# A streaming encoder step: order of dense and modulation quarters in the first feed-forward, and a new sum of the modulation rows

## The reference

```python
mod = jax.nn.silu(c) @ w + b                 # w: (2048, 6 * 2048) for each layer
...
x = x + gate1 * mix
h = rms_norm(x, g_ffn[i]) * (1.0 + scale2) + shift2
x = x + gate2 * ((silu(h @ w_gate[i]) * (h @ w_up[i])) @ w_down[i])
```

## Time and profile before

| What | Value |
|---|---|
| Time, median of 3 runs | 3439.44 us (3436.16 to 3441.07) |
| Profiled execution: its time, its span | 3440.21 us, 3438.4 us |
| Busy: TensorE, VectorE, ScalarE, GpSimd | 3290.4 (96%), 2095.9 (61%), 1309.0 (38%), 140.6 (4%) us |
| Mean granted clock of TensorE | 0.981 |
| Chain of work that ended last: TensorE, VectorE, DMA, ScalarE | 87%, 5%, 4%, 3% |
| First feed-forward | 983 to 2198 us |

### The profile page before, as it was taken

One profiled execution on the slowest core, in us unless ns is written; L12 is line 12 of the kernel. 1 busy time (PEld: TensorE's weight loads), 2 busy tenths in 40 slices (PEclk: granted clock), 3 DMA queues, 4 the chain that ended last, 5 costly groups with the idle time before them and its releaser, 6 DMA issues.

```text
span 3438.4 us, 48286 instructions
## 1 busy us (share of the span) xinstructions
PE 3290.4 (96%) x20405; PEld 2983.9 (87%) x20405; DVE 2095.9 (61%) x1804; ACT 1309.0 (38%) x991; POOL 140.6 (4%) x141
## 2 busy tenths in 40 slices
PE   7999998889989999999999999769999999999999
PEld 4677776667979999999999999659999999999999
DVE  3487885556887667676776767685444443334443
ACT  3344444455453443334433343334222232232221
POOL 0000000000000000000000000010000000000000
PEclk9999999999989999999999999889999999999999
DMA  9777767877645655556555555553433433333331
GB/s 353 272 259 241 246 241 250 294 273 262 221 166 175 208 203 180 186 183 209 194 178 188 195 203 187 181 187 134 130 126 122 130 126 122 131 125 122 124 132 62
DMA packets 325817, 646.50 MB, mean 188 GB/s; under 512 B 10882, under 2 KB 13514, under 8 KB 325322
## 3 DMA queue, kind: packets, MB, share of 16 engines
q1 hardware_dynamic: 317144, 630.17, 53.6%
q10 hardware_dynamic: 8586, 15.09, 1.2%
HBM read 631.46 MB, written 14.74 MB: 188 GB/s over the span
## 4 chain that ended last, share of the span: by engine, by line
PE 87%; DVE 5%; DMA 4%; ACT 3%; issue 1%; POOL 0%; SPq 0%; ACTq 0%; DVEq 0%; POOLq 0%
PE bank L1501 23%; PE bank L1503 23%; PE bank L1502 23%; PE bank L1583 3%; PE bank L1528 3%; PE bank L1584 3%; PE bank L1585 3%; DMA raw<-in_w_ada 3%; PE bank L1688 1%; PE bank L1537 1%; PE bank L1513 1%; PE bank L1716 1%; DMA raw<-in_cache_k 0%; PE bank L1717 0%; DVE w_lo L955 0%
## 5 line engine op out<-in xcount | busy, mean ns | idle before, releaser
L955 DVE TENSOR_TENSOR w_lo<-raw,w_hi 128x2048 fp32r<-128x2048 f32 x323 | 739.1, 2291 | 901.5 <-ACT w_hi L578 901.5
L578 ACT ACTIVATE w_hi<-raw 128x2048 fp32r<-128x2048 f32 x323 | 616.1, 1914 | 1373.3 <-PE bank L1503 1180.3
L1501 PE MATMUL bank<-h_hi,w_hi 128*128 128x384 f32 x3136 | 1064.1, 339 | 31.9 <-DVE h_lo L1034 24.0
L1502 PE MATMUL bank<-h_lo,w_hi 128*128 128x384 f32 x3136 | 1052.4, 336 | 0.0
L1503 PE MATMUL bank<-h_hi,w_lo 128*128 128x384 f32 x3120 | 1048.0, 336 | 0.0
L1501 PEld LDWEIGHTS bank<-h_hi,w_hi 128*128 128x128 f32 x3136 | 592.2, 189 | 77.1 <-issue 68.7
L1502 PEld LDWEIGHTS bank<-h_lo,w_hi 128*128 128x128 f32 x3136 | 592.4, 189 | 0.0
L1503 PEld LDWEIGHTS bank<-h_hi,w_lo 128*128 128x128 f32 x3120 | 589.0, 189 | 0.0
L1501 PE MATMUL bank<-act_hi,w_hi 128*128 128x384 f32 x1408 | 473.0, 336 | 0.0
L1503 PE MATMUL bank<-act_hi,w_lo 128*128 128x384 f32 x1408 | 470.5, 334 | 0.0
L1502 PE MATMUL bank<-act_lo,w_hi 128*128 128x384 f32 x1408 | 470.5, 334 | 0.0
(11 more groups left out here) (226 smaller groups left out, 2530.6 us busy)
## 6 DMA issues: line engine op xcount, KB each, us to landing
raw<-in_w_ada SPq DMA_DIRECT2D x192, 1024.0 KB, 5.9
raw<-in_w_gate SPq DMA_DIRECT2D x88, 1024.0 KB, 5.2
raw<-in_w_up SPq DMA_DIRECT2D x88, 1024.0 KB, 5.2
raw<-in_w_down SPq DMA_DIRECT2D x88, 1024.0 KB, 5.1
raw<-in_w_qkv SPq DMA_DIRECT2D x40, 1024.0 KB, 5.2
raw<-in_cache_k SPq DMA_DIRECT2D x32, 1024.0 KB, 6.3
raw<-in_cache_v SPq DMA_DIRECT2D x32, 1024.0 KB, 7.8
raw<-in_w_o SPq DMA_DIRECT2D x15, 1024.0 KB, 5.1
```

The lines of the kernel that those rows point to most:

```text
L578: act.activation(w_hi[:, s], raw[:, s], ACT.Copy).then_inc(hi_ready, 1)
L955: dve.tensor_tensor(w_lo[:, s], raw[:, s], w_hi[:, s].bitcast(f32), ALU.subtract).then_inc(lo_ready, 1)
L1501: pe.matmul(out, w, a, start=start, stop=False)
L1502: pe.matmul(out, w, al, start=False, stop=False)
```

## The change

In the first feed-forward, the eight quarters of gate and of up come in the order dense, dense, modulation, modulation (twice), where they came dense, modulation in turn. So slots 0 and 1 hold dense quarters and slots 2 and 3 modulation quarters; the last dense up quarter is unit 13, where it was unit 14. `paired` takes the place of `mixed`, and the waits that name units follow.

In all stages, the turn of the partial rows is four transposes of 128 x 128 (`ident`), where it was four matmuls with 9 columns. VectorE then sums the four groups, and in three-piece blocks the three pieces (`tensor_reduce`, 432 elements a partition, or 144 for the early and pooling blocks), waits for that, and adds the bias. `fold` and `fold3` and the GpSimd instructions that write them go. The four units ahead of the feed-forward, in the output projection and the norm, follow the new order.

```diff
@@ SyncE, order of the transfers
             def load_mixed(W, c, layer, a):
                 for i, w in enumerate((w_gate, w_up)):
-                    for j in range(4):
-                        load_pair(W + 2 * i, j, rows(w[0, j * 512:(j + 1) * 512, ds(c * 512, 512)]), layer, a + i)
+                    for n in range(8):
+                        j = 2 * (n // 4) + n % 2
+                        dense = rows(w[0, j * 512:(j + 1) * 512, ds(c * 512, 512)])
+                        load(*unit(W + 2 * i, n), dense if n % 4 < 2 else ada_src(layer, a + i, j))
                 load_down(W + 4, 0, c)
@@ GpSimd, at the start
-            do(pool.memset(fold[:], 0.0))
-            do(pool.memset(fold3[:], 0.0))
-            for j in range(4):
-                do(pool.affine_select(out=fold[:], in_=fold[:], compare_op=ALU.not_equal, fill=1.0,
...
@@ ScalarE (VectorE has the same with lo and mid)
+            def paired(W, n):
+                W, s = unit(W, n)
+                if s < 2:
+                    hi(W, [s])
+                else:
+                    top(W, [s])
...
             def mixed_chunk(W, c, a, following, last=False):
                 for n in range(4, 10):
-                    mixed(W, n)
-                gate_out(4 * W + 7)
-                mixed(W, 10); mod_out(4 * W + 8, a, 3); mixed(W, 11)
+                    paired(W, n)
+                gate_out(4 * W + 6)
+                paired(W, 10); mod_out(4 * W + 8, a, 3); paired(W, 11)
                 for n in range(12, 16):
-                    mixed(W, n)
+                    paired(W, n)
                 dense(W, 16); dense(W, 17)
                 for m in range(4):
                     acts_hi(c, m)
@@ VectorE
-            def mod_in(a, t_bank, part=None):
+            def mod_in(a, t_bank, part=None, pieces=3):
                 m = ds(4 * (a if part is None else part), 4)
                 dve.wait_ge(ada_t, a + 1)
+                parts = bank[:, t_bank, :].rearrange("p (m j q) -> p m j q", m=4, j=4)[:, :, :, 0:pieces * NC]
+                if pieces == 1:
+                    step.mark(dve.tensor_reduce(modA[:, m, :], parts.rearrange("p m j c -> p m c j"), AX.X, ALU.add))
+                else:
+                    step.mark(dve.tensor_reduce(modA[:, m, :], parts.rearrange("p m j (r c) -> p m c j r", r=pieces), AX.XY, ALU.add))
+                own()
                 bias = par[:, m].unsqueeze(2).to_broadcast([P, 4, NC])
-                dve.tensor_tensor(modA[:, m, :],
-                                  bank[:, t_bank, 0:4 * NC].rearrange("p (k c) -> p k c", k=4),
-                                  bias, ALU.add).then_inc(ada_done, 1)
+                dve.tensor_tensor(modA[:, m, :], modA[:, m, :], bias, ALU.add).then_inc(ada_done, 1)
...
             def mixed_chunk(W, c, a, layer, r, following, last=False):
                 for n in range(4, 12):
-                    mixed(W, n)
+                    paired(W, n)
                 mod_in(a, 4)
                 for n in range(12, 16):
-                    mixed(W, n)
+                    paired(W, n)
                 dense(W, 16); dense(W, 17)
-                times_up(c, 4 * W + 15)
+                times_up(c, 4 * W + 14)
                 dense(W, 18)
                 mod_in(a + 1, 3)
@@ TensorE
-            def ada_turn(a, t_bank, weights=fold3):
+            def ada_turn(a, t_bank):
...
                 for t in range(4):
-                    last = pe.matmul(bank[:, t_bank, t * NC:(t + 1) * NC], mod[:, t * P:(t + 1) * P], weights[:], start=True, stop=True)
+                    last = pe.transpose(bank[:, t_bank, t * P:(t + 1) * P], mod[:, t * P:(t + 1) * P], ident[:])
                 last.then_inc(ada_t, 1)
...
@@ TensorE, mixed_chunk
-                    to_features(W, 2 * j, 4, h_hi, h_lo, 4 * j, j == 0, j == 3, second_half=None if j else hr + 1)
-                    if j == 0:
+                    to_features(W, 4 * (j // 2) + j % 2, 4, h_hi, h_lo, 4 * j, j == 0, j == 3, second_half=None if j else hr + 1)
+                    if j == 1:
                         pe.wait_ge(residual_taken, r)
-                    ada_sub(W, 2 * j + 1, a, j, 3)
+                    if j % 2:
+                        ada_sub(W, 2 * j, a, j - 1, 3)
+                        ada_sub(W, 2 * j + 1, a, j, 3)
...
                 ada_turn(a, 4)
-                ada_sub(W, 9, a + 1, 0, 7)
-                for j in (1, 2):
-                    to_features(W, 8 + 2 * j, 0, h_hi, h_lo, 4 * j, False, False)
-                    ada_sub(W, 9 + 2 * j, a + 1, j, 7)
-                up_tail(W, 14)
+                to_features(W, 9, 0, h_hi, h_lo, 4, False, False)
+                ada_sub(W, 10, a + 1, 0, 7)
+                ada_sub(W, 11, a + 1, 1, 7)
+                to_features(W, 12, 0, h_hi, h_lo, 8, False, False)
+                up_tail(W, 13)
+                ada_sub(W, 14, a + 1, 2, 7)
                 ada_sub(W, 15, a + 1, 3, 7)
```

More of the change, by code:

```diff
@@ L149, in encoder_step @@
         mask, _ = nxt("mask", [P, 512])
-        fold, _ = nxt("fold", [P, NC])
-        fold3, _ = nxt("fold3", [P, NC])
         mod, _ = nxt("mod", [P, 512])
@@ L633, in norm_apply @@
                     for s in BETWEEN[n][g]:
-                        (mixed if n == 1 else dense)(W, s)
+                        (paired if n == 1 else dense)(W, s)
                     norm_tiles(n, 4 * g, 4, g + 2)
@@ L832, in _ @@
                 for n in range(6, 10):
-                    mixed(W, n)
+                    (paired if i == 3 else mixed)(W, n) if n >= 8 else mixed(W, n)
                 if i < 3:
@@ L887, in _ @@
             with act.Fori(0, CHUNKS - 1) as c:
-                mixed_chunk(W_FFN0 + c * 5, c, ADA_FFN + c * 2, mixed)
+                mixed_chunk(W_FFN0 + c * 5, c, ADA_FFN + c * 2, paired)
             mixed_chunk(W_FFN0 + 5 * (CHUNKS - 1), CHUNKS - 1, ADA_FFN + 2 * (CHUNKS - 1), dense, last=True)
@@ L975, in dense, with paired @@
                 lo(W, [s])
-            def mod_in(a, t_bank, part=None):
+            def paired(W, n):
+                W, s = unit(W, n)
+                if s < 2:
+                    lo(W, [s])
+                else:
+                    mid(W, s)
+            def mod_in(a, t_bank, part=None, pieces=3):
                 m = ds(4 * (a if part is None else part), 4)
                 dve.wait_ge(ada_t, a + 1)
+                parts = bank[:, t_bank, :].rearrange("p (m j q) -> p m j q", m=4, j=4)[:, :, :, 0:pieces * NC]
+                if pieces == 1:
+                    step.mark(dve.tensor_reduce(modA[:, m, :], parts.rearrange("p m j c -> p m c j"), AX.X, ALU.add))
+                else:
+                    step.mark(dve.tensor_reduce(modA[:, m, :], parts.rearrange("p m j (r c) -> p m c j r", r=pieces), AX.XY, ALU.add))
+                own()
                 bias = par[:, m].unsqueeze(2).to_broadcast([P, 4, NC])
-                dve.tensor_tensor(modA[:, m, :],
-                                  bank[:, t_bank, 0:4 * NC].rearrange("p (k c) -> p k c", k=4),
-                                  bias, ALU.add).then_inc(ada_done, 1)
+                dve.tensor_tensor(modA[:, m, :], modA[:, m, :], bias, ALU.add).then_inc(ada_done, 1)
             def norm_coef(n, k0=0, tiles=KT):
@@ L1115, in _ @@
             dve.wait_ge(par_ready, 1)
-            mod_in(0, 7, FIRST[0])
+            mod_in(0, 7, FIRST[0], 1)
             dve.wait_ge(rs_done, 1)
@@ L1122, in _ @@
                 if g:
-                    mod_in(i, 7, FIRST[i]); early(i)
-                mod_in(i + 1, 7, FIRST[i + 1])
+                    mod_in(i, 7, FIRST[i], 1); early(i)
+                mod_in(i + 1, 7, FIRST[i + 1], 1)
                 norm_coef(0, 4 * g, 4)
@@ L1413, in dense_chunk @@
                         rows_out(s)
-            with loop(dve, 0, CHUNKS - 1, {step: 4 * ADD}) as c:
-                mixed_chunk(W_FFN0 + c * 5, c, ADA_FFN + c * 2, 0, R_FFN0 + c * 4, mixed)
+            with loop(dve, 0, CHUNKS - 1, {step: 4 * ADD + 2}) as c:
+                mixed_chunk(W_FFN0 + c * 5, c, ADA_FFN + c * 2, 0, R_FFN0 + c * 4, paired)
             mixed_chunk(W_FFN0 + 5 * (CHUNKS - 1), CHUNKS - 1, ADA_FFN + 2 * (CHUNKS - 1), 0, R_FFN0 + 4 * (CHUNKS - 1), dense, last=True)
@@ L1479, in _ @@
                 if j % 2:
-                    mod_in(ADA_POOL + j // 2, 3)
+                    mod_in(ADA_POOL + j // 2, 3, pieces=1)
                 if j >= 3 and j % 2:
@@ L1611, in _ @@
             pe.wait_ge(par_ready, 1)
-            ada_turn(0, 7, fold)
+            ada_turn(0, 7)
             pe.wait_ge(xT_dve, 6)
@@ L1619, in _ @@
             ada_block(1, 6)
-            ada_turn(1, 7, fold)
+            ada_turn(1, 7)
             def early(d, turn=None):
@@ L1628, in early @@
                     if k == 2 and turn is not None:
-                        ada_turn(turn, 7, fold)
+                        ada_turn(turn, 7)
                     kt = 4 * j + k
@@ L1941, in _ @@
                 if j % 2:
-                    ada_turn(ADA_POOL + j // 2, 3, fold)
```

(1 more changed line is left out.)

## The result

The changed kernel takes 3486.12 us (median of 4 runs, 3480.70 to 3492.09), the kernel before 3437.80 (4 runs): a ratio of 1.0139, 95% interval 1.012 to 1.0159. It is slower, by 48 us; forecast were 3499, with a range of 3463 to 3515 (the forecast's own, without the rivals, was 3488 to 3508). The profiled execution took 3492.09 us with a span of 3490.3, 51.9 more than the one of before; forecast +59.9.

What follows compares the result with a forecast made beforehand. TensorE was taken as the bound. Against the profiled 3440.2 us, -22 - 4.8 + 55 + 26.4 + 2 + 3.3 = +59.9 gave 3500, forecast as 3499; own range 3488 to 3508, with rivals 3463 to 3515.

Steps and rivals of the forecast that it cites:

- The new wait: First feed-forward, ahead of unit 16: TensorE waits 5.0 us a chunk for activations behind unit 17's conversion, 55 us in all.
- U: Start of the chain after unit 13: when the next matmul would start, 0.17 us after the last start.
- Rival 2: Border of unit 13 and unit 16: unit 17's conversion doesn't hold the activations; -21.5 us, 3418; chance 0.07.
- The clock after the wait: Behind each chunk's wait TensorE runs at half clock: 2.4 us a chunk, 26 us, bounds nothing and 32.
- rival 1: In the chunks the wait is there but the clock stays up: 3473 us; chance 0.10.
- Merged blocks and turns: First feed-forward: paired modulation blocks save switches and transposes shorten turns, 2.0 us a chunk, 22 us for 11.
- rival 4: Turns on TensorE: transposes take 0.27 us each, 0.7 us more on 34 turns, 3523 us; chance 0.03.
- Twelve other turns: Nine turns in the projections and three in the output projection save 0.40 us each, 4.8 us.
- Order in the norm: Norm before the feed-forward: one more VectorE instruction ahead of h_lo, and a block no longer free: +3.3 us, once.
- The sum on VectorE: Reductions add 0.65 and 0.35 us, hidden in chunks; before projections, attention and in pooling mixer +2 us, between 0 and 4.
- rival 3: Up projection's fourth tile: waits for ScalarE's copy of the modulation rows, 1.3 us a chunk more, 3513 us; chance 0.08.
- The start and DMA: Start of the kernel and weight transfers: 18 fewer GpSimd instructions and reordered 1 MB transfers cost nothing.

Runs made afterwards that it cites:

- the filled wait: Changed kernel with 26 idle matmuls of 384 columns added in each chunk's wait ahead of unit 16: 3465.63 us, ratio 1.0081 to the kernel before.
- the kernel without gaps: Changed kernel with ScalarE and VectorE converting unit 17 behind the activations, not ahead of them: 3409.74 us, ratio 0.9922 to the kernel before.
- the order alone: New order of quarters with unit 17 converted behind the activations, and the old turn put back: 3428.70 us, ratio 0.9970 to the kernel before.
- the turn alone: Kernel before with only the transposes and VectorE's sum, in the old order of quarters: 3421.76 us, ratio 0.9953.
- the wait alone: Kernel before with one line making ScalarE wait for the last up quarter ahead of unit 17: 3527.01 us, ratio 1.0258.
- the one other order that was run: Kernel with unit 17 behind the activations, and units 2 and 3 moved behind the norm's last scaling step: 3410.45 us, ratio 0.9921.

## Why the prediction was right, step by step

- *The range*: 3486 lies in the range of 3463 to 3515, which the rivals set, but 2 us under the forecast's own 3488 to 3508. The two terms named for its lower end, 0.2 us less for the clock and 0.3 on the chain in each of 11 chunks, give 3493 and not 3488. The median is 13 us under 3499: 8 of them stand between the two traces and are taken apart below, the others are executions (the profiled one of the changed kernel is the slowest of its four, and the median of before is 1.6 lower with a fourth run).
- *The new wait*: forecast 5.0 us a chunk and 55 in all; measured 4.98 and 54.8. The chain from U (1634.41) to TensorE at 1641.00 is 6.59, forecast 6.55; the cover 1.61, forecast 1.55. Rival 2 (unit 17 doesn't hold the activations) fell, and the kernel with unit 17 moved is what it described: 3410, where it gave 3418.
- *The clock after the wait*: **the term that was mis-sized.** Forecast 2.4 us a chunk, 26.4 in all; measured 20.5 by the filled wait. The drop came behind eleven of eleven gaps, so rival 1 fell, but the running at half clock behind a restart was 2.9 to 6.1 us (mean 4.2), where the two restarts of the earlier trace rows lasted 4.6 and 6.1. At 47% lost, single chunks lose 1.3 to 2.8 us. I had taken the shortest of six restarts of before as the lower end. They were too few for that, and the trace of before has a shorter one that I passed over: 3.4 us at half clock from 824.15 (in the rows further down).
- *Merged blocks and turns*: 22 forecast, 23.5 measured in the kernel without gaps, where a chunk takes 107.48 us (forecast 107.5). Their split was off by 1 us: a chunk takes 108.39 with the order alone, 13.5 us saved in 11 chunks where 14.3 stood, and 108.81 with the turn alone, 8.8 where 7.7 stood. Another 1.2 come only with both.
- *Transposes at their single duration* (rival 4): the trace's row of twelve was the better guide. Four take 0.36 us at a granted clock of 1.00, though each shows 0.27 of duration. By the Trainium skill ("TensorE: Matmul & The Clock Gate", Part 4: PE-mode transpose), at about 275 ns each, they would have taken 1.1; its figure agrees with the duration in the trace, and not with the distance between starts, which is what counts here. What that section says of transposes and the clock, no run here tests.
- *Twelve other turns*: forecast 4.8, measured 4.7 in the projections and 3.3 in the output projection, 8.0. Of these, 2.9 are the clock and not the change. In both kernels TensorE waits 2.6 us in the projections and 1.3 us in the output projection for VectorE's remainder. Here are the stretches behind these two gaps, in the kernel before and then in the changed one (columns as above, the clock third from the end):

```profile
176.23:182.40 6.17, 6.17 (x15) 4.82 (x16) 5.39 (x3) 2.51 (x2) 0.00 (x0) 0.50 0.91 295
823.59:827.60 4.01, 4.01 (x14) 4.01 (x15) 3.98 (x2) 2.80 (x2) 0.00 (x0) 0.57 1.01 331
```
```profile
175.25:178.45 3.20, 3.20 (x8) 2.52 (x9) 2.42 (x2) 2.52 (x2) 0.00 (x0) 0.50 0.83 227
820.10:824.10 4.00, 4.00 (x23) 4.00 (x24) 3.96 (x2) 2.91 (x2) 0.00 (x0) 1.00 0.90 297
```

The first restart ran at half clock for 6.2 us before and 3.2 after, worth 1.4 us; the second for 3.4 us before and not at all after, worth 1.5. The kernel with the old turn and the new order has the shorter first and no second stretch too, so it isn't the turn that spares them. The other 5.1 are thirteen turns at 0.39: nine, three, and the one behind the last block of the output projection. Against it stands the attention between them, which the change does not touch: 2.4 us longer in this execution, between 3.3 shorter and 0.1 longer in the six other kernels with the new turn, whose program is the same up to there. That is variation of the executions.
- *Order in the norm*: forecast +3.3, measured +2.6 from the output projection's last turn to the quarter behind the wait for h_lo, and 1.0 more in the chunks for the block that stood in that wait and no longer does. The wait grew from 4.16 to 7.79 us.
- *The sum on VectorE*: an addition of 0.65 and 0.35 us was forecast, the two reductions take 0.60 and 0.30 us. It is hidden in the chunks, which have no wait for it. Ahead of attention TensorE waits 1.20 us for VectorE, where it waited 0.56. What it cost in the pooling mixer can't be told: from the norm behind the feed-forward to the last matmul the changed kernel takes 1.0 us longer than the kernel before, but the order alone and the wait alone, which have the old turn, take 1.8 and 1.5 longer.
- *A second wait at the fourth tile* (rival 3): no gap between gate and up in any chunk. ScalarE goes from conversion to table load, SiLU, conversion and copy as the rival said, and the copy of the modulation rows starts 6.4 us after the first conversion and takes 0.59, inside the 7.8 that TensorE needs to come there.
- *The start and DMA*, forecast at nothing: the first matmul comes 0.3 us earlier, the projections begin 1.0 earlier, and no gap of TensorE in the chunks is put down to a load.

The sum, from trace to trace: between the quarter behind the wait for h_lo and the norm behind the feed-forward, +54.3 was measured. The gaps of 54.8, less 23.5 for blocks and turns, plus the 1.0 of the block that now stands there, leave 22.0 for the clock; eleven restarts of 4.2 us, of which 47% is lost, make the same, and the filled wait gave 20.5. With +2.6 in the norm and -5.6 elsewhere it is +51.3 to the last matmul. Of the 8.6 us by which the forecast of +59.9 was above that, 4.4 are the clock, 1.5 the blocks and turns, and the rest the terms outside the feed-forward, where 2.9 us of shorter half clock helped, which the forecast did not have.

## What to carry to other kernels

When the order of units in a ring changes, list for each unit whose slot it takes and when that one is used last; a conversion that was free to run ahead may now wait, and on an engine with a strict order everything behind it waits as well. Then look at what stands behind it: here moving two lines turned 1.4% slower into 0.8% faster than before. A gap is to be priced with the half clock that may follow it, and where an engine's queue was full (VectorE in the norm, 39.54 of 40.34 us), the one other order that was run only moved the wait.

## What the runs showed of the hardware

- GpSimd's subtraction of two SBUF operands all but stood still while VectorE's subtraction of two SBUF operands ran: 2.70 us instead of 1.00, and 4.03 for two, ending 0.87 and 0.88 us behind VectorE. With VectorE's subtraction held back, all of them took 1.0 us again. VectorE's products, which read one operand from PSUM, did not hold it: four of them run until 1640.71 in the changed kernel beside an `act_lo` from 1639.95, and all four `act_lo` take 3.91. The Trainium skill ("SBUF — State Buffer", Who interferes with whom) says that an instruction of VectorE with two SBUF inputs contends with one of GpSimd that reads SBUF, and that the order in which the two were issued decides which one blocks. The runs agree: both times VectorE's subtraction had begun before the `act_lo` that it held.
- The length of a gap alone did not decide the clock: of gaps of 2.04 us it fell behind 3 of 11, of 3.74 behind 11 of 11, of 4.98 behind 11 of 11. Behind a gap of 1.26 us in the output projection it fell in the kernel before, and behind one of 1.28 at the same place it stayed in the changed one. In the kernel before, 2.67 us of idle time did not lower it.
